# Thirty-two bytes more in each slot of two weight rings: a decoder layer on one core

## What is computed

```python
u = rms_norm(x, g_mix);  z = u @ w_in                      # 1024 x 4512
y_a = MLA(z) @ w_proj_mla;  y_r = Retention(z) @ w_proj_ret
h = x + (sigmoid(g_A) * y_a + sigmoid(g_R) * y_r) @ w_out
h = h + CrossAttn(rms_norm(h) @ w_xq, rms_norm(mem) @ w_xkv) @ w_xo
a, b = causal_dwconv3(rms_norm(h) @ w_up)                  # 1024 x 2816 each
h = h + (silu(a) * b) @ w_down
return rms_norm(h, g_final)
```

## Time and profile before

| | |
|---|---|
| median of 2 runs | 2058.49 us (2056.86 to 2060.11) |
| the profiled execution | 2060.93 us, its span 2059.1 us |
| PE busy | 1926.0 us, 94% of the span |
| POOL / DVE / ACT busy | 844.3 / 920.7 / 557.6 us |
| mean granted TensorE clock | 0.972 of full speed |

### The profile page before, as it was taken

One profiled execution on the slowest core, in us unless ns is written; L12 is line 12 of the kernel. 1 busy time (PEld: TensorE's weight loads), 2 busy tenths in 40 slices (PEclk: granted clock), 3 DMA queues, 4 the chain that ended last, 5 costly groups with the idle time before them and its releaser, 6 DMA issues.

```text
span 2059.1 us, 25536 instructions
## 1 busy us (share of the span) xinstructions
PE 1926.0 (94%) x9308; PEld 1605.1 (78%) x9308; DVE 920.7 (45%) x1522; ACT 557.6 (27%) x988; POOL 844.3 (41%) x324
## 2 busy tenths in 40 slices
PE   5999999999978888899999889999999999999997
PEld 4888888888767776778778778787888788878876
DVE  5454540000166666453431543666146516741664
ACT  5222231100245555211223421422022202210223
POOL 4333334566320001244326134455655564555451
PEclk9999999999979999999999999999999999999998
DMA  4111112233110002532114112111211121112112
GB/s 152 42 31 31 35 47 92 82 95 107 43 31 1 1 1 66 194 120 102 42 41 134 51 49 84 42 51 51 62 51 51 51 62 51 47 55 62 51 48 85
DMA packets 35339, 128.39 MB, mean 62 GB/s; under 512 B 4032, under 2 KB 4160, under 8 KB 35264
## 3 DMA queue, kind: packets, MB, share of 16 engines
q1 hardware_dynamic: 25776, 92.72, 14.9%
q10 hardware_dynamic: 9488, 34.61, 4.4%
HBM read 110.54 MB, written 16.78 MB: 62 GB/s over the span
## 4 chain that ended last, share of the span: by engine, by line
PE 76%; DVE 9%; issue 6%; ACT 5%; DMA 2%; POOL 1%; SPq 0%; ACTq 0%; DVEq 0%; POOLq 0%
PE ps L309 23%; PE ps L314 23%; PE ps L315 23%; PE ps L588 3%; POOL wl L284 1%; ACT prow L1016 1%; PE ps L567 1%; ACT pr L1177 1%; DVE p1l L1268 1%; DVE t L1271 1%; DVE amax L1541 1%; DMA xs<-in_x 1%; DVE ul L1271 1%; DVE yb L1775 1%; PE ps L383 0%
## 5 line engine op out<-in xcount | busy, mean ns | idle before, releaser
L291 POOL TENSOR_SCALAR wh<-raw 128x1024 fp32r<-128x1024 f32 x152 | 429.9, 2828 | 1105.5 <-PE ps L309 910.0
L293 POOL TENSOR_TENSOR wl<-raw,wh 128x1024 fp32r<-128x1024 f32 x152 | 376.3, 2475 | 12.7
L309 PE MATMUL ps<-uh,wh 128*128 128x512 f32 (+1 forms) x576 | 229.3, 398 | 3.3 <-DVE ul L1271 3.3
L315 PE MATMUL ps<-uh,wl 128*128 128x512 f32 (+1 forms) x576 | 226.3, 393 | 0.0
L314 PE MATMUL ps<-ul,wh 128*128 128x512 f32 (+1 forms) x576 | 226.2, 393 | 0.0
L309 PE MATMUL ps<-fah,wh 128*128 128x512 f32 x352 | 139.5, 396 | 9.0 <-DVE fal L1268 6.6
L315 PE MATMUL ps<-fah,wl 128*128 128x512 f32 x352 | 138.4, 393 | 0.0
L314 PE MATMUL ps<-fal,wh 128*128 128x512 f32 x352 | 138.4, 393 | 0.0
L309 PE MATMUL ps<-f0h,wh 128*128 128x512 f32 x352 | 137.0, 389 | 1.3 <-DVE z L1759 1.3
L309 PE MATMUL ps<-f1h,wh 128*128 128x512 f32 x352 | 137.7, 391 | 0.3 <-DVE f1l L1271 0.3
L315 PE MATMUL ps<-f1h,wl 128*128 128x512 f32 x352 | 137.7, 391 | 0.0
(11 more groups left out here) (347 smaller groups left out, 4128.2 us busy)
## 6 DMA issues: line engine op xcount, KB each, us to landing
raw<-in_slabs SPq DMA_DIRECT2D x168, 512.0 KB, 3.6
xs<-in_x SPq DMA_DIRECT2D x8, 512.0 KB, 7.6
s_ga<-sig ACTq DMA_DIRECT2D x8, 512.0 KB, 2.6
s_mr<-mxr ACTq DMA_DIRECT2D x8, 512.0 KB, 5.0
xtile<-in_x ACTq DMA_DIRECT2D x8, 512.0 KB, 6.1
sab<-s_ga ACTq DMA_DIRECT2D x8, 512.0 KB, 4.2
mrb<-s_mr ACTq DMA_DIRECT2D x8, 512.0 KB, 5.2
s_h<-hT ACTq DMA_DIRECT2D x8, 512.0 KB, 2.6
```

Source lines behind the costliest of these rows:

```text
L291: pool.tensor_scalar(wh[:, j, :], raw[:, j % RAWS, :], 1.0, None, ALU.mult).then_inc(S["w_hi"], 1)
L293: pool.tensor_tensor(wl[:, j, :], raw[:, j % RAWS, :], wh[:, j, :].bitcast(f32), ALU.subtract).then_inc(S["w_ready"], 1)
L309: l = pe.matmul(o, lh, rh, start=start, stop=False)
L315: return pe.matmul(o, ll, rh, start=False, stop=stop)
```

## The change

```diff
+APART = 8
@@
-        sb("line_up_slabs", [P, 96])
         raw = sb("raw", [P, RAWS, 1024])
-        wh = sb("wh", [P, SLOTS, 1024], f32r)
-        wl = sb("wl", [P, SLOTS, 1024], f32r)
+        wh = sb("wh", [P, SLOTS, 1024 + APART], f32r)
+        wl = sb("wl", [P, SLOTS, 1024 + APART], f32r)
@@
-        sb("line_up_tiles", [P, 80])
+        sb("line_up_tiles", [P, 112])
@@ split() of POOL
-                    pool.tensor_tensor(wl[:, j, :], raw[:, j % RAWS, :], wh[:, j, :].bitcast(f32),
+                    pool.tensor_tensor(wl[:, j, 0:1024], raw[:, j % RAWS, :], wh[:, j, 0:1024].bitcast(f32),
@@
-                pool.tensor_scalar(wh[:, j, :], raw[:, j % RAWS, :], 1.0, None, ALU.mult).then_inc(S["w_hi"], 1)
+                pool.tensor_scalar(wh[:, j, 0:1024], raw[:, j % RAWS, :], 1.0, None, ALU.mult).then_inc(S["w_hi"], 1)
@@ ACT, the slabs of w_xkv
-                copy(wh[:, j % SLOTS, :], raw[:, j % RAWS, :]).then_inc(S["w_kv_hi"], 1)
+                copy(wh[:, j % SLOTS, 0:1024], raw[:, j % RAWS, :]).then_inc(S["w_kv_hi"], 1)
```

## The result

The changed kernel takes 2096.24 us in the median (2093.17 to 2099.31) against 2058.49 us before: a ratio of 1.0193, 95% interval 1.0156 to 1.0231. Each median is of two runs. It is slower, by about 38 us. That lies inside the stated range, but the forecast was no effect at all, and what came is the loss that Rival A names.

The account below looks back on a forecast made before the run. The prediction took PE's matmul rate, 226.7 ns per 512 columns, as the bound. All parts summed to 0 on the profiled 2060.93 us, forecast as 2058.5 us on the median of runs; range 2042 to 2103 us.

Parts of the forecast that it names:

- Rival A: Matmuls out of the ring lose the steady step, 233.3 ns each: 2101 us, bound 2143; chance 0.17 in full, 0.05 in part.
- the 13.3 ns: Part of each matmul's step beyond one column per cycle at 2.4 GHz, claimed the same at any length; at most 85 us.
- the first part of the sum: Stationary operands loaded from new remainders beside the stream: cost 0, bounds +85 and -85 us over 6,384 matmuls.
- the `ident_r` rows: Loads of `ident_r` from remainder 352 beside `kbh` at 0: median 188 ns, stream step 0.23 us, taken as showing no cost.
- The key expansion: Second test: heads 2 and 3 load 64 columns from remainders 0 and 256, both 0.24 us apart, taken as no effect.
- The price of 43 us: Rival A's cost: 6.7 ns more on each of 6,384 matmuls, from the rope key's 233.3 ns steps.
- Rival B: Equal remainders make PE's two readers collide and the change cures it: up to 85 us gained, 1973 us; chance 0.11, smaller part 0.05.
- Rival C: Multiples of 32 bytes are the wrong grid, so nothing moves: same time as forecast; chance included in the 0.62 for no effect.
- Second part: POOL, DVE, ACT and DMA writing slots and tiles while PE reads: nothing to part, cost 0 and no gain.
- Third part: POOL's speed on `raw`, `wh`, `wl` at other remainders: 0; a tenth slower would cost +4 us in memory keys and values.
- Fourth part: Transfers into `raw` from remainder 128: taken as 0, bound 3 us either way on 16 slabs; skill's page estimate +4 us.
- Fifth part: Query and value rows, where the ring is the moving operand: 120 matmuls, 9 ns each would be 1 us.

Follow-up runs that it names:

- e3: Kernel before with both weight rings and all large tiles moved to remainder 128, slots not padded; 2059.81 us, ratio 1.0012.
- e6: Kernel before with slots padded by 16 elements, slot j at 64 j in the high ring and 256 + 64 j in the low; 2073.2 us, one time.
- e11: Kernel before with only the low ring moved, to remainder 256; 2058.83 us, ratio 1.0002.
- e2: Kernel before with both rings at remainder 128, all slots alike, no padding, large tiles at 0; 2090.68 us, ratio 1.0156.
- e8: Kernel before with the rope key's weight blocks 512 bytes apart instead of 128, all at remainder 0, still 32 columns each; 2063.04 us, one time.
- e1: Kernel before with only the two `raw` buffers moved to remainder 128, both rings at 0; 2059.82 us, ratio 0.9999.

## Why the prediction was right or wrong

The time landed inside the range by luck. The range reached up into Rival A, but the forecast was no effect on PE's rate, and that is wrong. The count was right: 6,384 matmuls out of the ring, and one nanosecond on each about 6.4 us. The reading of the 13.3 ns as a rest that is the same at every length, and as the only place where addresses could act, does not hold after the change: with 512 columns the step grows by 6.7 ns, with 384 (query rows, the ring moving) from 173.6 to 175.4 ns, back at 173.6 in e3, and with 256 it falls by about 1 ns.

The step that failed is the first part of the sum, "Between these ends I take 0, because the `ident_r` rows are the nearest". The rows were read rightly, but they could not show the effect. A load at another distance does not get longer, as the total of the loads shows, PEld 1605.1 us in both pages: it is the start of the next matmul that moves, by 6.7 ns. A single row in hundredths of a microsecond cannot tell that: 0.23 us fits 226.7 ns and 233.3 ns alike. The row also had nothing to be compared with, as `ident_r` is loaded only in short bursts and stood 96 bytes (modulo 256) from `kbh` already before; no run put it in line. The key expansion of the earlier trace rows was no test either: its two distances, 0 and 256, are the same modulo 256, as e6 and e11 show. What the runs show in place of the 0 is 233.3 ns for 226.7 in the steady step (e2 against e3). The prediction named the weakness of the `ident_r` rows in its last sentence and still gave Rival A only 0.17 in full and 0.05 in part.

Rival A named the right loss in the right place (233.3 ns in place of 226.7), but its reason was wrong and its price near by luck. The step is not unsettled: slab after slab repeats at 233.3 ns as it did at 226.7, and what sets it is the distance between two operands, not the remainder of one. The price of 43 us, against 38.4 us of span, came from the rope key. That stays high in e8 with all blocks at distance 0 and falls to 229.3 ns in the changed kernel, so it is no measure of this effect; that both gave 233.3 ns is a coincidence. The rest of the difference is that the mean to start from is 227.15 ns, not 226.7, because the steps after a restart cost more already before.

Rival B was right that the two operands' places matter to each other, and wrong about the cure: the kernel before already stood at the cheapest distance of all that were tried, and none gives back any of the 13.3 ns. The Trainium skill's rule that PE never waits on anyone and has two independent read ports (SBUF — State Buffer, "Who interferes with whom") was used against both rivals; the runs disagree with it for these operands, since e3 against e2 leaves the rings where they are, moves the tiles behind them by 128 bytes, and takes the time from 1.0156 of the kernel before to 1.0012. What inside the memory or PE makes the distance count, the runs do not show. Lines of 32 bytes that repeat after eight would fit the steps at 16, 32 and 256 bytes, but not the exception at 192, and that was only argued.

Rival C did not hold: multiples of 32 bytes are just what counts.

Second part (writers): e1, with DMA writing and POOL reading at another remainder, changes nothing; POOL's writes into the rings could not be moved without the rings, but e3 moves them by 128 bytes at no cost. Third part: right for the two rows that it named, POOL's high part 2814 ns after 2828, L284 2394 ns after 2389. The low part of L293 went from 2475 to 2540 ns, hidden while POOL waits for PE; as it is at 2530 ns in e8 too, where no ring or tile is moved, and at 2520 to 2540 ns in every other run, the addresses are not what made it longer. Fourth part: right, 3.6 us; the estimate of +4 us for a start off 256 bytes was not seen, e1 being at 0.9999 with an upper end of 1.0016, 3.3 us. Fifth part: right in size, the query rows lose under 2 ns a matmul. The shares had a slip of no weight: the range also leaves out most of the smaller part of Rival B (0.05), which it does not say.

## What to carry to other kernels

Where a stream of float32 matmuls with 512 columns moving and 128 loaded runs without a gap at 2.4 GHz, read its step from the distance of starts, over many steps. Start the weights that are loaded at the same place, modulo 256 bytes, as the activations that stream by; here that was worth 6.7 of 233.3 ns. A lead of 16 bytes was free too; places a few bytes below, and starts other than 0 and 128 for the activations, were not tried, nor was the lower clock. One odd tensor between the weights and the activations, or padding meant to spread slots, shifts the distance for all of them at once. Rows of the same operation in short bursts are no evidence for what a steady stream will do.

## What was not expected

The cost is a step and not a slope: 0 at 16 bytes, all of it at 32, and one exception at 192 (228.9 ns). Matmuls with 256 columns do not pay it: in the memory keys and values the mean of their distances under 150 ns went from 119.8 ns before (338 of them) to 118.9 ns after (329). And at distance 0 the step of 512 columns is longer with 32 stationary columns, 231.7 ns in e8, than with 128, 226.7 ns, though a quarter as much is loaded. There a distance even helps, 229.3 ns in the changed kernel. Why the cost depends on the columns in this way, no run shows.
